# One 2 MB weight load of a mixture-of-experts kernel, issued in sixteen parts of eight rows

## The reference: what is computed

```python
def expert_block(args):
    xb, e = args
    gu = xb @ w_gate_up[e] + b_gate_up[e]
    gate, up = gu[..., :D_FF_EXPERT], gu[..., D_FF_EXPERT:]
    gate = jnp.minimum(gate, SWIGLU_LIMIT)
    up = jnp.clip(up, -SWIGLU_LIMIT, SWIGLU_LIMIT)
    act = (up + 1.0) * gate * jax.nn.sigmoid(SWIGLU_ALPHA * gate)
    return act @ w_down[e] + b_down[e]
```

## Time and profile before

| | us |
|---|---|
| median of 3 runs | 1194.3 (1193.4 to 1194.74) |
| profiled execution, its time | 1193.76 |
| its span | 1191.9 |
| PE busy (share of the span) | 1112.3 (93%) |
| DVE busy | 350.1 (29%) |
| ACT busy | 166.9 (14%) |

### The profile page before, as it was taken

The page is one execution under the profiler, slowest core; times in us unless marked ns, Lnnn a source line. Parts: engine busy times, 40 slices in busy tenths (PEclk is TensorE's granted clock), DMA queues, the critical chain, the costliest instruction groups (busy, mean ns, idle before and its releaser), DMA issues.

```text
span 1191.9 us, 15326 instructions
## 1 busy us (share of the span) xinstructions
PE 1112.3 (93%) x6538; PEld 542.0 (45%) x6538; DVE 350.1 (29%) x738; ACT 166.9 (14%) x272; POOL 4.0 (0%) x23
## 2 busy tenths in 40 slices
PE   6999999999999999999898799998799898989897
PEld 5889886764434343433343334333334333333332
DVE  3685244453213212212121122222212222121213
ACT  3431233441101000010101000101010101010002
POOL 1000000000000000000000000000000000000000
PEclk9999999999999999999999899999899999999899
DMA  9832324677999999999999999999999999999994
GB/s 338 300 122 91 129 83 116 253 280 302 429 429 426 427 429 432 428 431 429 431 430 427 428 428 431 429 432 427 428 430 428 429 430 431 430 428 432 429 425 178
DMA packets 39052, 436.03 MB, mean 366 GB/s; under 512 B 5813, under 2 KB 5898, under 8 KB 20330
## 3 DMA queue, kind: packets, MB, share of 16 engines
q1 hardware_dynamic: 37082, 433.68, 86.7%
q10 hardware_dynamic: 1904, 1.33, 0.6%
HBM read 433.95 MB, written 1.05 MB: 365 GB/s over the span
## 4 chain that ended last, share of the span: by engine, by line
PE 68%; DMA 27%; issue 2%; DVE 1%; ACT 1%; SPq 0%; DVEq 0%; PEldq 0%
DMA ring<-in_w_down 26%; PE ps L1950 22%; PE ps L1990 16%; PE ps L1534 4%; PE ps L2005 4%; PE ps L1639 4%; PE ps L1920 3%; PE ps L1585 3%; PE ps L1516 3%; PE ps L1635 2%; PE ps L1696 2%; PE ps L1772 1%; PE ps L1816 1%; PE ps L1940 1%; DMA ring<-in_w_in 1%
## 5 line engine op out<-in xcount | busy, mean ns | idle before, releaser
L1990 PE MATMUL ps<-ring,work 128*64 128x512 f32 x1024 | 241.1, 620 | 28.8 <-DMA ring<-in_w_down 24.6
L1950 PE MATMUL ps<-work 128*64 128x512 f32 x1024 | 234.6, 601 | 0.2 <-DVE work L1382 0.2
L1950 PE MATMUL ps<-ring,work 128*64 128x512 f32 x1024 | 227.2, 597 | 6.2 <-DMA ring<-in_w_gate_up 6.1
L1990 PEld LDWEIGHTS ps<-ring,work 128*64 128x64 f32 x1024 | 79.5, 142 | 166.1 <-issue 155.8
L1950 PEld LDWEIGHTS ps<-ring,work 128*64 128x64 f32 x1024 | 72.9, 138 | 155.7 <-issue 143.3
L1950 PEld LDWEIGHTS ps<-work 128*64 128x64 f32 x1024 | 74.0, 139 | 138.8 <-issue 132.2
L1415 DVE COPY work<-ps 128x512 f32<-128x512 f32 x16 | 11.1, 691 | 241.5 <-PE ps L1516 241.5
L1392 DVE TENSOR_SCALAR work<-ps 128x512 f32<-128x512 f32 x32 | 21.9, 686 | 195.9 <-PE ps L1516 195.9
L1427 DVE COPY work<-ps 128x512 f32<-128x512 f32 (+1 forms) x16 | 11.1, 691 | 206.3 <-PE ps L1990 206.3
L786 ACT ACTIVATE ps<-work 128x512 f32<-128x512 f32 x32 | 19.3, 602 | 364.9 <-DVE work L1392 364.9
L2005 PE MATMUL ps<-work 128*128 128x512 f32 (+1 forms) x132 | 59.7, 608 | 10.4 <-ACT work L793 10.2
(11 more groups left out here) (235 smaller groups left out, 722.0 us busy)
## 6 DMA issues: line engine op xcount, KB each, us to landing
work<-in_w_gate_up SPq DMA_DIRECT2D x64, 2048.0 KB, 35.3
ring<-in_w_gate_up SPq DMA_DIRECT2D x24, 4096.0 KB, 32.2
ring<-in_w_down SPq DMA_DIRECT2D x22, 4096.0 KB, 35.4
ring<-in_w_down SPq DMA_DIRECT2D x19, 2048.0 KB, 21.8
ring<-in_w_gate_up SPq DMA_DIRECT2D x16, 2048.0 KB, 19.7
ring<-in_w_in SPq DMA_DIRECT2D x7, 2048.0 KB, 15.6
ring<-in_xattn_w_kv SPq DMA_DIRECT2D x2, 2048.0 KB, 14.3
ring<-in_w_out SPq DMA_DIRECT2D x2, 2048.0 KB, 8.0
```

Source lines behind the costliest of these rows:

```text
L1950: last = nc.tensor.matmul(bank(b)[p], xg_T[k][:, kb, :], quad_columns(w[:, kk, D_MODEL * (q // 2):D_MODEL * (q // 2 + 1)], q % 2), start=F ...
L1990: last = nc.tensor.matmul(bank(Y_BANK + y)[p], act_T[k][:, b, HALF * c:HALF * c + HALF], w[:, b, 512 * q:512 * q + 512], start=False, stop ...
```

## The change

The load of chunk (13, 0) is no longer one transfer of 128 rows but sixteen of eight rows each, one behind the other on the same queue, to the same place and from the same addresses. Each raises the semaphore of place 6 by 16, so TensorE's counts for place 6 go up by 15 loads from pair 13 on. Nothing else is changed: the same bytes, the same order, the same wait of SP ahead of the first of them.

```diff
+BY_EIGHTS = (13, 0)
+SHARES = 16
...
+        def loads_by_eights(i, s):
+
+            return SHARES - 1 if i >= BY_EIGHTS[0] and s == chunk_place(*BY_EIGHTS)[0] else 0
+
         def loads_before(i, c):
...
-            return uses_before_experts(s) + use
+            return uses_before_experts(s) + use + loads_by_eights(i, s)
...
-                sp.dma_start(place(s), src).then_inc(S(f"slot_loaded{s}"), 16)
+                if isinstance(i, int) and (i, c) == BY_EIGHTS:
+                    n = P // SHARES
+                    for r in range(SHARES):
+                        sp.dma_start(place(s)[n * r:n * r + n], src[n * r:n * r + n]) \
+                            .then_inc(S(f"slot_loaded{s}"), 16)
+                else:
+                    sp.dma_start(place(s), src).then_inc(S(f"slot_loaded{s}"), 16)
```

More of the change, by code:

```diff
@@ L383, in loads_in_first_pass @@
         def loads_in_first_pass(s):
-            return uses_before_experts(s) + len([1 for i in range(PAIRS) for c in range(PAIR_CHUNKS)
-                                                 if chunk_place(i, c)[0] == s and first_pass_chunk(i, c)[1] is not None])
+            return uses_before_experts(s) + loads_by_eights(PAIRS, s) + len(
+                [1 for i in range(PAIRS) for c in range(PAIR_CHUNKS)
+                 if chunk_place(i, c)[0] == s and first_pass_chunk(i, c)[1] is not None])
         def later_pass_place(c):
```

## The result

| | before | after |
|---|---|---|
| median, us | 1194.03 (1193.4 to 1194.74, 4 runs) | 1215.15 (1212.81 to 1217.2, 4 runs) |
| ratio after / before | | 1.0181, interval 1.0169 to 1.0193 |
| profiled execution, its time | 1193.76 | 1213.55 |
| its span | 1191.9 | 1211.8 |

The change makes the kernel 1.8% slower, 21.1 us by the medians and 19.8 us between the two profiled executions. The direction was forecast, the size was not: 1201 was said, with 1190 to 1214 as the range, and the median lies 1 us above that range.

A forecast was written before the change was run, and what follows sets the result against it. The stream of loads was taken to bound the kernel until 1108 us. Crowding of 19.6 - 4.9 = 14.7 us less 8.3 us of lead gave 6.4 us; 1193.76 + 6.4 + 0.5 = 1200.7, said as 1201, range 1190 to 1214.

The forecast's parts named there:

- What bounds the kernel: Up to the landing at 1108.13 us the stream of loads sets the time; lateness there reaches the end in full.
- The issues: SP at chunk (13, 0): sixteen issues take 4.5 to 5.4 us, ending near 973 with 9 us to spare; cost zero.
- Which engines carry eight rows: Each of the sixteen new transfers uses eight engines, one 16 KB row on each; likeliest always the same eight.
- The lead: Eight engines run about 8.3 us ahead; they likeliest take the chunk, so 8.3 us comes off the extra work.
- What the eight engines need for it: Chunk (13, 0) on eight engines: 19.6 us at a taken 107 GB/s, between 9.8 and 40, where 4.9 were before.
- the forecast's 6.4 us: How much later the stream of loads runs: 14.7 us more on the eight engines, of which 8.3 is lead.
- The new waits: TensorE in pair 13: some 2.7 us at chunks 1 and 2, about 4 at 1034.74; DMA share below 1 after 992.
- The second: Rival: the eight engines behind take the chunk, no lead to spend; 1199 without crowding, 1209 with it; chance 0.13.
- the third: Rival: full crowding, one transfer after the other at 53 GB/s, 27 us later, 1221; chance 0.05.
- The first rival: The lead is spent and nothing crowds: stream 3.4 us earlier, 1191; needs over 159 GB/s; chance 0.25.
- The fourth: Rival: the sixteen transfers spread over all engines in turn, each carrying its 4.9 us as before; 1194; chance 0.07.

The follow-up runs named there:

- the run with low spread rows: Against the kernel before: chunk (13, 0) as eight transfers of every fourth row, rows 0 to 63 only, the other 1 MB left out; 1192.99 us, ratio 0.9995.
- Doubling the chunk: Sixteen transfers of eight rows, every fourth row, at chunk (14, 0) as well as (13, 0); 1224.63 us, ratio 1.0263 to the kernel before.
- rows 64 to 127 alone: Chunk (13, 0) as eight transfers of every fourth row, rows 64 to 127 only, the other 1 MB left out; 1202.16 us, ratio 1.0072 to before.
- the spread version: The changed kernel, but each of the sixteen transfers takes eight rows four apart, in on-chip memory and source; 1208.58 us, ratio 1.0131 to before.
- low and high alone: The changed kernel with only the eight transfers of neighbouring rows for rows 0 to 63, or for 64 to 127, 1 MB left out; 1201.95 and 1209.66 us.

## Why the prediction was wrong, step by step

**What bounds the kernel** held. The stream of loads sets the time, and what it loses before the landing of 1108 arrives at the end: 20.5 us at the landing, 19.9 at the end of the span. TensorE's clock added nothing to the sum, as said. It does fall behind the new waits: the granted clock is 0.64 and 0.68 from 1005 to 1015 and 0.50 from 1035 to 1040, and the 32 matmuls there take 8.89 and 10.01 us where 7.1 stood. But slower matmuls only shorten the next wait, since the landing ends it anyway: the waits grew by 15.5 us and these matmuls by 4.7, 20.2 together, against 20.5 at the landing.

**The issues** held: 5.38 us inside the stated 4.5 to 5.4, no instruction of SP later, cost zero.

**Which engines carry eight rows** held: eight engines, by the 112 closing packets, and the same eight every time, by the eight chains of the run with low spread rows.

**The lead** is the step that failed. The forecast set 8.3 us against the extra work, because the eight engines that carry the chunk were taken to be the eight that are ahead. No row of before said so, and they are not: six of them are, and two belong to those behind, by the chains at 990.0 to 991.0 and at 996.2 and 996.5 us. A landing waits for its last engine, so nothing could be set against the cost. Doubling the chunk showed this without relying on the reading of shares.

**What the eight engines need for it** failed too, in its kind more than in its size. The term priced the crowding as time of the eight engines, 19.6 us, of which 4.9 they had before, so 14.7 more. The runs show a rate that falls for all sixteen, the transfer ahead in the queue included, and it falls once for each group's turn, even when the group is two engines. For the spread rows the sum is then: 4.9 us for the rows that two engines without lead carry in addition, and two turns at half rate that lose 4.9 each, 14.7 in all; 15.6 were measured. With rows 64 to 127 alone nobody carries more than before, and twice 4.9 is 9.8; 8.6 were measured. (The forecast had 14.7 before it subtracted the lead, too; it came out of a guessed rate, and that the two agree is chance.) For the change itself the missing bytes, 16.6 us, and the 4.9 make 21.5, and 21.1 were measured (this only says that the page's bytes and the time agree; the 16.6 are not derived); the 5.5 us above the spread version are what neighbouring rows add. So a lead that was not there took 8.3 us from the sum, and the neighbouring rows put 5.5 on it. With both, the forecast's 6.4 us would be 20.2. For the runs with 64 rows in a transfer this sum is about 5 us too low (9.8 against 14.7, and 2.5 against 7.7), so it is not yet a rule for all shapes.

**The new waits** came in part at the wrong place, and the DMA share, which was to fall below 1, stayed there; the forecast had allowed for more busy time for fewer bytes, and that is what came, over 35 us and not 10. Pair 13 waits 4.79 us at the chunks 1 and 2, where 2.7 was said, and 1.47 us at the chunks 5 and 6, where 4 was said: 6.3 in all, as forecast. But the largest, 8.24 us, stands in pair 12, before the chunk is used, for weights that the forecast took to be out of reach because they were issued before it.

**The rivals.** The second, that the eight behind take it, was named with 1209 and a chance of 0.13, and is nearest to what happened in its mechanism: no lead to spend, with the wrong count of engines. The spread version, 1208.6, lands beside its number, by another sum. In time alone the third (1221, chance 0.05) is as near to 1215, with full crowding but the lead still taken off. The range ended at 1214 since no case had both the missing lead and a crowding beyond that of 107 GB/s. The first rival needed a rate over 159 GB/s for the eight; the run of spread low rows shows that such a rate exists (eight engines with 128 KB each in 4.9 us, 214 GB/s), but for rows that these engines seem to write anyway. The fourth, even work and no change, fell with the same chains: eight engines carry all of it.

**One reading for all of it.** What the runs share is this, if the eight engines are those of rows 0 to 63: it costs nothing where each engine writes the rows that are its own in a transfer of 128 rows, and it costs where it writes beside another engine's rows. Low spread rows on the eight low engines: no cost. High spread rows, and rows 0 to 63 on sixteen engines: about half rate, 8.6 and 7.7 us. Eight neighbouring rows: eight engines close together, and even the low half costs 8.5 us. The Trainium skill has this as a port of 27.2 GB/s for each set of eight rows ("SBUF — State Buffer", section "Door 1: The DMA port swizzle") and the order in which engines take them in a transfer of 128 rows ("DMA: Bandwidth & Descriptors", section "The descriptor swizzle"); by these, rows four apart are eight ports and eight neighbours are two. The runs agree for the direction of every case. Sharing a port accounts by itself only for the engines that share it; here all sixteen were halved, also when only two engines wrote the high rows. The forecast quoted the first page and used it as a price for the eight engines alone. The Trainium skill also says, in "DMA: Bandwidth & Descriptors", section "Back-pressure in remote DMA", that a full port holds up every engine that shares its path; that is written of transfers between cores, and here local loads showed as much: fourteen engines slowed by two, and a transfer ahead in the queue later by 9.6 us.

**Open.** That all sixteen are held up is shown; by what path is not. With neighbouring rows the halves are not additive: low and high alone cost 8.5 and 16.2, with 4.9 for the extra rows 29.6, and both together 21.1. Why transfers of 64 rows lose some 5 us more than two turns at half rate is open too. And why the engines are not level, and two of those that carry the eights are behind, was not tried. (That six of the others are behind with them follows from the half of the engines that ends last in the earlier trace rows.) No version was found that beats the kernel before: to relieve the engines behind, others would have to write their rows, and in every run here that did so the rate fell.

## What to carry to other kernels

In this stream of loads 2 MB cost least with 128 rows in one transfer. Cutting them by columns was free here, cutting them by rows cost 14 to 25 us in 1194, even into halves of 64. A DMA share at 1 is no proof of a full stream; look at the GB/s beside it. And a lead of some engines may be counted only when it is shown that the engines with the lead are the ones that get the work, all of them, since the last one sets the landing.

## What the runs showed of the hardware that was not expected

Two engines that write rows 64 to 127 double the time of every other engine's packets (2.49 to 2.57 us for 32 KB in place of 1.22). Two transfers of 64 rows in place of one of 128 cost 14.7 us for 2 MB that take 4.9 at full rate. One transfer of 64 rows on sixteen engines cost 7.7 us where eight transfers of eight spread rows with the same bytes cost nothing (1201.23 against 1192.99 us). A transfer slows down what is ahead of it in the queue: the 4 MB issued 0.5 us earlier landed 42.8 us after their issue in place of 33.2. Sixteen issues of 128 rows x 1 KB kept SP for 33.21 us, against 5.38 for sixteen of eight rows x 16 KB. And the sixteen engines fall into those ahead and those behind by some 8 us after 870 us of loads, with the division not along the eight that carry the eights: two of these are behind, and they end last in the kernel after and in the runs with spread rows.
